# Convolution tap 0 moved from VectorE to ScalarE, and one cast of q moved to the tick before

## The reference

```python
p = rmsnorm(x) @ w_in            # columns: q | k | v | z | xbc | dt
# group A: 16 heads of dilated sliding-window attention (softmax(q k + bias) v)
# group B: causal depthwise convolution of width 4 on xbc, then silu, then the SSD scan
def causal_conv(xbc, prior, conv_w, conv_b):
    t = xbc.shape[1]
    xpad = jnp.concatenate([prior, xbc], axis=1)
    out = sum(xpad[:, i:i + t] * conv_w[i] for i in range(CONV_WIDTH)) + conv_b
    return jax.nn.silu(out), xpad[:, t:]
```

## Time and profile before

| | |
|---|---|
| median of 3 runs | 2114.23 us |
| profiled execution, own time | 2109.64 us |
| its span in the trace | 2107.8 us |
| mean granted TensorE clock | 0.984 |
| TensorE, VectorE, ScalarE, GpSimd busy over the span | 95%, 49%, 33%, 45% |
| the interleaved stage | about 333 to 850 us |

### The profile page before, as it was taken

The page is one execution under the profiler, slowest core; times in us unless marked ns, Lnnn a source line. Parts: engine busy times, 40 slices in busy tenths (PEclk is TensorE's granted clock), DMA queues, the critical chain, the costliest instruction groups (busy, mean ns, idle before and its releaser), DMA issues. The chain is left out here.

```text
span 2107.8 us, 30132 instructions
## 1 busy us (share of the span) xinstructions
PE 1999.7 (95%) x11992; PEld 1817.8 (86%) x11992; DVE 1029.6 (49%) x1355; ACT 699.6 (33%) x1194; POOL 944.8 (45%) x580
## 2 busy tenths in 40 slices
PE   8999999988888999799988999999999999999999
PEld 7999998777777888465556789999999999999998
DVE  5888703877767665477767552521212122121212
ACT  5344323666656765455542011210010101010010
POOL 4688514767757664334333123242333333233332
PEclk9999999999999999799998999999999999999999
DMA  4444425344343443678745433111111111111112
GB/s 167 156 183 159 158 103 132 106 121 105 93 100 102 128 121 109 232 253 276 239 178 192 171 110 124 40 51 40 51 40 50 40 50 40 44 45 49 41 50 92
DMA packets 117925, 239.36 MB, mean 114 GB/s; under 512 B 29995, under 2 KB 63659, under 8 KB 116284
## 3 DMA queue, kind: packets, MB, share of 16 engines
q1 hardware_dynamic: 94956, 205.69, 30.7%
q10 hardware_dynamic: 22864, 32.25, 4.7%
HBM read 187.78 MB, written 58.67 MB: 117 GB/s over the span
## 5 line engine op out<-in xcount | busy, mean ns | idle before, releaser
L913 POOL TENSOR_SCALAR att_p<-att_p,att_rden 128x128 f32<-128x128 f32 (+7 forms) x128 | 251.0, 1968 | 130.0 <-DVE att_rden L1053 129.9
L2101 POOL CAST wo_hi<-wo_raw 128x1024 fp32r<-128x1024 f32 x64 | 66.7, 1042 | 494.1 <-issue 241.6
L2425 ACT ACTIVATE r_sq<-stage 128x1056 f32<-128x1056 f32 x32 | 34.8, 1088 | 625.6 <-DVE stage L2614 625.6
L2103 POOL TENSOR_TENSOR wo_lo<-wo_raw,wo_hi 128x1024 fp32r<-128x1024 f32 x64 | 187.3, 2926 | 5.1
L1058 DVE TENSOR_TENSOR att_pTlo<-att_t_ps,att_pThi 128x512 fp32r<-128x512 f32 x192 | 106.3, 554 | 109.1 <-ACT att_pThi L1173 107.7
L1173 ACT ACTIVATE att_pThi<-att_t_ps 128x512 fp32r<-128x512 f32 x192 | 93.2, 486 | 123.8 <-PE att_t_ps L995 116.6
L966 PE MATMUL dense_ps<-u_hi,w_hi 128*128 128x352 f32 x480 | 115.9, 343 | 16.3 <-DVE conv_pre L1085 7.8
L673 DVE RECIPROCAL proj_rinv<-proj_rinv 128x1056 f32<-128x1056 f32 x16 | 108.0, 6753 | 9.9 <-ACT proj_rinv L563 9.9
L2624 DVE TENSOR_TENSOR h<-h,wo_psa 128x1056 f32<-128x1056 f32 x32 | 40.2, 1255 | 144.2 <-PE wo_psa L2341 144.2
L1165 ACT ACTIVATE att_p<-att_p,att_min 128x128 f32<-128x128 f32 (+7 forms) x128 | 98.7, 772 | 32.0 <-DVE att_min L1071 31.0
L966 PE MATMUL dense_ps<-u_lo,w_hi 128*128 128x352 f32 x480 | 108.9, 336 | 0.0
(11 more groups left out here) (325 smaller groups left out, 5511.6 us busy)
## 6 DMA issues: line engine op xcount, KB each, us to landing
sa_k<-in_cache_k SPq DMA_DIRECT2D x32, 640.0 KB, 7.9
sa_v<-in_cache_v SPq DMA_DIRECT2D x40, 512.0 KB, 4.7
w_raw<-in_w_feat SPq DMA_DIRECT2D x36, 512.0 KB, 6.3
wo_raw<-in_w_up SPq DMA_DIRECT2D x32, 512.0 KB, 3.5
wo_raw<-in_w_down SPq DMA_DIRECT2D x32, 512.0 KB, 3.5
out_qk<-proj_out SPq DMA_DIRECT2D x16, 528.0 KB, 7.9
tmp_bias_rows<-tmp_table ACTq DMA_DIRECT2D x8, 1024.0 KB
att_bias<-tmp_bias_rows SPq DMA_DIRECT2D x16, 512.0 KB, 3.3
```

The source lines that it names most:

```text
L913: pool.tensor_scalar(slot(h, qt), slot(h, qt), rden[:, qt, :], None, ALU.mult).then_inc(normed, 1)
L2103: pool.tensor_tensor(w_lo[:, j], raw_w, w_hi[:, j].bitcast(F32), ALU.subtract).then_inc(f_split[j], 1)
```

## The change

Tap 0 leaves VectorE's list and becomes a ScalarE activation of function Identity with the tap weight as scale and the bias as bias, both taken per partition from the `taps` tile, after the casts and before the tanh of its tick. It takes its three waits with it, and one more (`halved`, set once at the start). The planner no longer counts tap 0 in the VectorE load. The cast of the low part of q goes from ticks with n mod 12 = 3 to those with n mod 12 = 2, right behind the second half of the high part.

```diff
@@ planner
             for t, n in enumerate(sorted(free)):
                 tap_at.setdefault(n, []).append((d, t))
-                busy[n] += 1.3
+                busy[n] += 1.3 if t else 0.0
                 last = n
@@ VectorE
             def convolve(d, t):
                 w = taps[:, d, t:t + 1]
-                if t == 0:
-                    dve.wait_ge(evicted, 3 * (d + 1))
-                    dve.wait_ge(padded, d + 3)
-                    if d >= 1:
-                        dve.wait_ge(feat_stored, stores(d))
-                    dve.tensor_scalar(half[:, 0:CONV], pre[:, 0:CONV], w, taps[:, d, WIDTH:WIDTH + 1], ALU.mult,
-                                      ALU.add).then_inc(conv, 1)
-                else:
-                    dve.wait_ge(conv, WIDTH * d + t)
-                    dve.scalar_tensor_tensor(out=half[:, 0:CONV], in0=pre[:, t:t + CONV], scalar=w,
-                                             in1=half[:, 0:CONV], op0=ALU.mult, op1=ALU.add).then_inc(conv, 1)
+                dve.wait_ge(conv, WIDTH * d + t)
+                dve.scalar_tensor_tensor(out=half[:, 0:CONV], in0=pre[:, t:t + CONV], scalar=w,
+                                         in1=half[:, 0:CONV], op0=ALU.mult, op1=ALU.add).then_inc(conv, 1)
...
                 for d, t in tap_at.get(n, ()):
-                    convolve(d, t)
+                    if t:
+                        convolve(d, t)
@@ ScalarE
+            def first_tap(d):
+                act.wait_ge(evicted, 3 * (d + 1))
+                act.wait_ge(padded, d + 3)
+                act.wait_ge(halved, 1)
+                if d:
+                    act.wait_ge(feat_stored, stores(d))
+                act.activation(half[:, 0:CONV], pre[:, 0:CONV], ACT.Identity, bias=taps[:, d, WIDTH:WIDTH + 1],
+                               scale=taps[:, d, 0:1]).then_inc(conv, 1)
...
                     if n % TICKS == 2:
                         cast_q(h, slice(HD, P))
-                    if n % TICKS == 3:
                         cast_q_low(h)
                     if n % TICKS == 8:
                         cast_v(h)
+                for d, t in tap_at.get(n, ()):
+                    if t == 0:
+                        first_tap(d)
                 for d in tanh_at.get(n, ()):
                     tanh(d)
```

## The result

The changed kernel takes 2120.88 us (median of 10 executions, 2116.82 to 2122.09), the kernel before 2114.08 beside it. The ratio is 1.0025, with a 95% interval of 1.0014 to 1.0036: 3 to 8 us slower, a little. The prediction of 2117.5 was 3.4 too low. The time lies in its range (2110.5 to 2122), but 0.9 above the likeliest case's own (A, 2115 to 2120) and close to case D's 2121.6. The profiled execution took 2120.21; that of before, 2109.64, was a quick one for its kernel, so of the 10.6 us between the two profiles about half is no effect of the change.

A forecast was written before the change was run, and what follows sets the result against it. The prediction took TensorE, busy 95% of the span, as the bound, so only its gaps count. Tile, cast and GpSimd terms sum to +3.3 on the profiled execution, giving a median of 2117.5 us, range 2110.5 to 2122.

The forecast's parts named there:

- A: The forecast itself as likeliest case: 2115 to 2120 us, chance 0.50.
- case D: Rival: TensorE feels all 4.0 of tile 4's keep_high delay and one new gap brings another slow-clock stretch; +7.4, 2121.6, chance 0.20.
- The low cast, -1.4 + 0.3: Five of 7 TensorE waits for q's low cast shrink by 0.28; late keep_low costs +0.1 and +0.2 in tiles 8, 9.
- Price of the tap: Tap 0 as a ScalarE activation over 1080 columns takes 1.28 us, against 0.848 on VectorE.
- Tiles without cost: In tiles 2, 3, 5, 6, 8, 9, 10 moving the tap costs nothing and brings nothing.
- tile 7's: The one exception among the cost-free tiles: keep_low comes 0.2 sooner, -0.2.
- Tile 0, +1.25: The tap delays ScalarE's casts and first invert; GpSimd passes the delay whole to w_lo, for which TensorE waits.
- Tile 1, +1.4: Tap and low cast delay keep_high in ticks 1 to 3, so bias_min of tile 0 reaches TensorE's score 1.4 late.
- Tile 4, +1.6: In tick 31 ScalarE stands 3.8 us for tile 3's store; keep_high, exponent and bias_min follow late, TensorE's score by 1.6.
- Tile 11, +0.75: In tick 110 high cast, low cast and tap stand together; keep_high comes 2.1 later and the score waits 0.75.
- GpSimd, -0.4: Four of twelve taps lie beside a GpSimd normalisation, some 0.4 longer there; one in four reaches TensorE.

The follow-up runs named there:

- f1: Kernel before with the low cast of q moved one tick ahead and, from head 1 on, cut to 8 of 1024 columns; 2109.35 us, ratio 0.9987.
- e2: Kernel before with only the low cast of q moved one tick ahead, tap 0 still on VectorE; 2118.43 us, ratio 1.0029.
- f2: Kernel before with the low cast moved in heads 7 and 8 only, tap 0 on VectorE; 2115.67 us, ratio 1.0013.
- e1: Changed kernel with the low cast back in its old tick, so only tap 0 moved to ScalarE; 2112.94 us, ratio 1.0008.
- e6: Changed kernel, but the gate is written to and stored from tanh's buffer, so tap 0 doesn't wait for the stores; 2114.54 us, ratio 1.0015.
- e7: Kernel before with tap 0 on VectorE cut to 8 of 1080 columns, nothing added on ScalarE; 2110.75 us, ratio 0.9990.
- f4: Changed kernel with the gate stored from tanh's buffer and the low cast moved only in heads 13 to 15; 2113.57 us, ratio 0.9995.
- f7: Kernel before with the low cast moved in all heads but 7 and 8, tap 0 on VectorE; 2112.64 us, ratio 1.0000.
- f6: Kernel before with the low cast in its old place, cut to 8 of 1024 columns from head 1 on; 2106.09 us, ratio 0.9963.
- f9_low_dve: Kernel before with the low cast on VectorE in tick 2 ahead of keep_low, tap 0 on VectorE; 2111.68 us, ratio 0.9996.

## Why the prediction was right or wrong

**Right in the total, and in part by luck.** The forecast was +3.3; the ratio gives +5.3 (3.0 to 7.6). That is past the likeliest case's own range and nearer to case D, which had a chance of 0.20. By halves, the terms of the tap (1.25 + 1.4 + 1.6 + 0.75 - 0.2 - 0.4 = +4.4) measured +1.7 (-1.5 to +4.9), so 4.4 isn't excluded, but the term of the cast (-1.1) measured +6.1 (3.6 to 8.7): wrong in size and in sign.

**The low cast, -1.4 + 0.3: the step that failed.** The wait fell from 4.5 to 3.1, as forecast, and in the two heads with an eviction behind the late keep_low TensorE waits for it, as the step said, with "no gain there, and +0.1 and +0.2". Both the size of that wait and its sequel were wrong. The eviction empties three banks one after the other, and all three matmuls of the next group wait for it: about 1.1 us in head 7, so +0.8 with the cast's 0.3 taken off (an estimate from f1's 2.11 us for before's 1.05). And the step has no term for the clock, which there falls to 1.2 GHz and costs another 1.4. From keep_low of tick 74 to that of tick 77 it is 8.17 us in the changed kernel, 8.15 in e2 and 8.22 in f2, for 6.01 before: +2.2 for a term of +0.1. In head 8, from tick 86 to tick 89, it is 9.64 in the changed kernel, 9.42 in e2 and 9.32 in f2, for 6.96 before; but e1, with the cast where it was, takes 9.00, so there the tap alone can bring most of it. Why the mean clock falls in f1, and not in e6, stays open.

**Price of the tap**: 1286 ns, forecast 1.28.

**Tiles without cost**: keep_low of ticks 48 to 66 of the changed kernel keeps its distance to that of before (6.5 us), but for the late keep_low of ticks 51 and 63, which is caught up by the next. The one gain, tile 7's, was forecast as -0.2 and is 0.24.

**Tile 0, +1.25**: TensorE's wait for w_lo is 1.71 for 1.11 and was to be 2.3. So half: +0.6 came through GpSimd. It is 1.7 in all five profiles with this tap on ScalarE and 1.1 in all nine others. Why the other half is lost wasn't tried.

```profile
361.96 0.43 PE L966 MATMUL dense_ps<-u_hi,w_hi 128*128 128x352 f32 x1 [1.71 <-POOL w_lo L228]
```

**Tile 1, +1.4**: the new wait for bias_min is there, 0.92 of the forecast 1 to 1.5:

```profile
374.41 0.44 PE L984 MATMUL att_s_ps<-att_k,att_qhi 128*128 128x384 f32 x1 [0.92 <-DVE att_min L1071]
```

Ticks 0 to 12 take 32.19 us for 30.16, but 31.96 also in f2 and 31.49 in e7, which change nothing of these ticks but, in e7, the length of the tap on VectorE. f2 has the same new wait too, 1.22, and before has none. One profile can't carry this term.

**Tile 4, +1.6: undersized, by the clock above all.** The mechanism is as described, ScalarE at the store, then keep_high, the exponent and the invert. ScalarE came there at 440.1 and not at 437.96, as everything was 2.2 later by then; the wait was 4.93 and not 3.8, since the store took 10.7 us to land and not 9.6. TensorE's waiting grew by about 2.0, near the forecast; the other 1.7 of the 3.7 us are the longer stretch at half clock, for which the sum had no term. Case D had one of just this size ("one new gap brings another such stretch (+1.7)"), but its "TensorE feels all 4.0" isn't borne out. In e1 the store landed sooner, and the same code paid nothing.

**Tile 11, +0.75**: keep_low's distance to before goes from 9.7 to 10.6 between ticks 110 and 112, +0.9. e6, which has tap and cast moved as well, shows the same, and e1, e2 and f4, which have one of the two, show nothing: it takes both, as the step said. The rest of the profile's rise up to tick 124 is clock (below).

**GpSimd, -0.4**: its normalisations took 248.8 us for 251.0, so 2.2 in all, and TensorE's share can't be seen. Versions with all 12 taps on VectorE and the cast on ScalarE lie between 249.4 (f7) and 251.4 (f6), so most of the 2.2 can be chance. The Trainium skill (GPSIMD Engine Reference, Specifications, with VectorE: DVE Perf Modes, Mode 2x_2P), as the prediction reads it, would have all 12 taps relieve GpSimd; these 2.2 us over twelve taps are 0.2 each, and no run here separates them from changes in overlap.

## What to carry to other kernels

Where TensorE is the bound, price an edit twice: by TensorE's waits, and by the clock behind them, which here cost as much again (tile 4, head 7). Look for waits inside merged rows too, by the time from one start to the next: the idle time in brackets showed 0.29 us where the eviction held TensorE 1.1. Ahead of an in-order engine's wait on a store, ask how much the landing time varies, not only when it was in one trace. And time each half of a two-part change by itself: a total can come out as forecast from terms that are both wrong.

## What the runs showed of the hardware

**The clock differs with the work the same.** In the changed kernel and in e6_store_from_th the order from tick 118 on is the same and TensorE has the same gap (1.56 and 1.58). First the windows of the changed kernel, then those of e6:

```profile
680.00:685.00 5.00, 5.00 (x25) 4.63 (x23) 1.50 (x5) 1.19 (x3) 4.13 (x3) 0.66 0.12 6
685.00:690.00 5.00, 3.44 (x24) 2.94 (x22) 3.45 (x8) 3.45 (x6) 1.27 (x2) 1.00 0.25 81
690.00:695.00 5.00, 4.99 (x20) 4.69 (x21) 2.12 (x3) 4.89 (x7) 3.43 (x3) 0.66 0.06 24
```

```profile
676.00:681.00 5.00, 5.00 (x30) 4.60 (x31) 2.34 (x7) 2.28 (x7) 4.12 (x3) 1.00 0.30 74
681.00:686.00 5.00, 3.42 (x21) 2.72 (x20) 3.73 (x8) 3.73 (x6) 2.80 (x2) 1.00 0.31 105
686.00:691.00 5.00, 5.00 (x32) 4.75 (x33) 1.85 (x2) 4.89 (x8) 2.94 (x3) 1.00 0.06 15
```

From keep_low of tick 118 to that of tick 130 it is 31.91 us in one and 28.97 in the other. Why the clock differs isn't shown. Steps of this size make a large part of the difference between executions of one kernel: over the 35 of the kernel before timed with e1 the clock lost has a standard deviation of 4.0 us, and the span one of 3.6. Only means over many executions show a change of 3 us.

**VectorE and GpSimd share a price, and who pays changes with the order.** In tick 3 of head 0 of the kernel before the tap on VectorE takes 1.50 and GpSimd's subtraction beside it 2.21; in e2, where the subtraction starts 0.05 ahead of the tap instead of 0.44 behind it, 2.39 and 1.29. The one that starts second is slowed; e1 and f7, where the subtraction also starts first, agree (2.17 and 1.28; 2.29 and 1.29). Before, then e2:

```profile
369.71 1.50 DVE L1111 SCALAR_TENSOR_TENSOR silu_half<-conv_pre,conv_taps,silu_half 128x1080 f32<-128x1080 f32 x1
...
370.15 2.21 POOL L228 TENSOR_TENSOR w_lo<-w_raw,w_hi 128x512 fp32r<-128x512 f32 x1
```

```profile
370.11 2.39 DVE L1111 SCALAR_TENSOR_TENSOR silu_half<-conv_pre,conv_taps,silu_half 128x1080 f32<-128x1080 f32 x1
...
370.06 1.29 POOL L228 TENSOR_TENSOR w_lo<-w_raw,w_hi 128x512 fp32r<-128x512 f32 x1
```

**The same cast varies on VectorE**: of the 15 casts of 64x1024 in f9_low_dve eight take 0.69 us and the others 0.74 to 1.39, 0.93 in the mean; on ScalarE it is 1.06 each time.
